# Where VectorE copies finished attention outputs out of PSUM, moved one step earlier in three attention loops

## The reference

```python
# latent attention: 8 heads, two query blocks of 128, causal
s = einsum('bqhd,bkhd->bhqk', q[:, lo:hi], k[:, :hi]) * scale
p = softmax(where(causal, s, NEG_BIG))
o = einsum('bhqk,bkhd->bqhd', p, v[:, :hi])

# cross attention, in each of the first two layers: 4 heads, 256 x 256, no mask
s = einsum('bqhd,bmhd->bhqm', q, k_mem) * MEM_HEAD_DIM ** -0.5
o = einsum('bhqm,bmhd->bqhd', softmax(s), v_mem)

# sparse attention (nsa): 16 heads, three branches summed under gates
out = gb[..., 0:1] * o_cmp + gb[..., 1:2] * o_slc + gb[..., 2:3] * o_win
```

## Time and profile before

| | us |
|---|---|
| median of three runs | 3019.53 |
| lowest, highest | 3018.77, 3023.99 |
| the profiled execution's own time | 3018.77 |
| its span, first to last instruction | 3017.1 |
| PE busy | 2875.0 (95%) |
| DVE busy | 2073.7 (69%) |
| ACT busy | 1501.7 (50%) |
| attention loops: latent | about 78 to 106 |
| cross attention, layers 0 and 1 | about 172 to 186 and 566 to 579 |
| nsa | about 2025 to 2093 |

### The profile page before, as it was taken

How to read it: one execution, slowest core, us unless ns; L and a number is a source line. 1 busy time by engine, 2 the same in 40 slices (tenths; PEclk the granted TensorE clock), 3 DMA queues, 4 the chain that set the end, 5 groups by cost and what they waited for, 6 DMA issues and landing times.

```text
span 3017.1 us, 52823 instructions
## 1 busy us (share of the span) xinstructions
PE 2875.0 (95%) x18004; PEld 2567.0 (85%) x18004; DVE 2073.7 (69%) x3647; ACT 1501.7 (50%) x2607; POOL 60.6 (2%) x118
## 2 busy tenths in 40 slices
PE   8889998899999899999999999999899999999998
PEld 6679787798799799999988888776899999988886
DVE  4567975689765678888965555525588879855555
ACT  2444444544534434448964555114344469845544
POOL 0000100011000000000000000000000000000000
PEclk9999999999999999999999999989999999999999
DMA  5439963499763455553345555540445542355553
GB/s 180 126 113 277 354 224 105 120 301 375 249 180 108 136 175 184 181 181 108 101 155 193 194 191 185 128 126 1 147 157 184 182 157 101 105 188 192 192 193 125
DMA packets 310916, 518.35 MB, mean 172 GB/s; under 512 B 37026, under 2 KB 209442, under 8 KB 310179
## 3 DMA queue, kind: packets, MB, share of 16 engines
q1 hardware_dynamic: 294402, 456.78, 47.7%
q0 software_dynamic: 16416, 60.30, 5.6%
HBM read 515.97 MB, written 1.05 MB: 171 GB/s over the span
## 4 chain that ended last, share of the span: by engine, by line
PE 83%; ACT 7%; DVE 4%; issue 3%; DMA 2%; ACTq 1%; SPq 0%; DVEq 0%
PE ps L915 33%; PE ps L846 11%; PE ps L842 11%; PE ps L843 10%; PE ps L893 3%; ACT spread L1869 1%; DMA tile_ring<-mlp_w_in 1%; ACT spread L1875 1%; PE ps L1282 1%; ACT hot_pair L1869 1%; PE ps L1404 1%; PE ps L817 1%; PE ps L1045 1%; PE ps L776 1%; ACT hot_pair L1875 1%
## 5 line engine op out<-in xcount | busy, mean ns | idle before, releaser
L842 PE MATMUL ps<-x_high,w_high 128*128 128x256 f32 x3264 | 815.9, 287 | 21.6 <-DVE x_low L2570 10.6
L843 PE MATMUL ps<-x_low,w_high 128*128 128x256 f32 x3264 | 804.6, 284 | 0.0
L2070 DVE TENSOR_TENSOR w_low<-tile_ring,w_high 128x1024 fp32r<-128x1024 f32 x360 | 441.1, 1225 | 326.1 <-ACT w_high L1701 325.0
L842 PEld LDWEIGHTS ps<-x_high,w_high 128*128 128x128 f32 x3264 | 628.4, 193 | 29.9 <-issue 15.2
L843 PEld LDWEIGHTS ps<-x_low,w_high 128*128 128x128 f32 x3264 | 629.4, 193 | 0.3
L1701 ACT ACTIVATE w_high<-tile_ring 128x1024 fp32r<-128x1024 f32 x360 | 382.5, 1062 | 473.7 <-PE ps L915 473.7
L846 PE MATMUL ps<-x_high,w_low 128*128 128x256 f32 x3264 | 460.5, 284 | 1.4 <-DVE w_low L2846 1.4
L1849 ACT ACTIVATE w_high<-tile_ring 128x1024 fp32r<-128x1024 f32 x256 | 270.1, 1056 | 314.8 <-PE ps L846 314.3
L846 PEld LDWEIGHTS ps<-x_high,w_low 128*128 128x128 f32 x3264 | 423.7, 193 | 1.6 <-DVE w_low L2846 1.6
L915 PE MATMUL ps<-w_high,x_high 128*128 128x512 f32 x1440 | 387.6, 391 | 21.1 <-DVE x_low L2064 21.1
L915 PE MATMUL ps<-w_high,x_low 128*128 128x512 f32 x1440 | 386.6, 390 | 0.0
(11 more groups left out here) (347 smaller groups left out, 3018.3 us busy)
## 6 DMA issues: line engine op xcount, KB each, us to landing
tile_ring<-peer_u SPq DMA_DIRECT2D x256, 512.0 KB, 3.3
tile_ring<-peer_v SPq DMA_DIRECT2D x256, 512.0 KB, 3.3
arena<-mod_w POOLq DMA_DIRECT2D x112, 512.0 KB, 5.7
tile_ring<-mlp_w_in SPq DMA_DIRECT2D x64, 512.0 KB, 5.1
tile_ring<-mlp_w_out SPq DMA_DIRECT2D x64, 512.0 KB, 5.5
tile_ring<-ret_w_in SPq DMA_DIRECT2D x48, 512.0 KB, 3.9
tile_ring<-peer_w_q SPq DMA_DIRECT2D x32, 512.0 KB, 4.0
tile_ring<-sb_w_qkv SPq DMA_DIRECT2D x24, 512.0 KB, 4.2
```

The costliest lines, as they stand in the source:

```text
L842: nc.tensor.matmul(dst, cols, x_high[:, c, :], start=c == 0, stop=False)
L843: nc.tensor.matmul(dst, cols, x_low[:, c, :], start=False, stop=False)
L2070: V.tensor_tensor(w_low[:, k % 2, :], tile_ring[:, k, :], w_high[:, k % 2, :].bitcast(F32), ALU.subtract).then_inc(low_ready, 1)
```

## The change

Three edits, all on VectorE's side. No instruction is added or removed; 20 lifts stand elsewhere in its stream.

```diff
             def attend(n, group, pre, post, out, lift=None):
 
                 for i in range(n + 3):
+                    if i >= 3 and (i - 3) % group == group - 1:
+                        lift_out(out(i - 3))
                     if i < n:
                         pre(i)
                     if 1 <= i <= n:
                         post(i - 1)
-                    if i >= 3 and (i - 3) % group == group - 1:
-                        lift_out(out(i - 3))
                     if lift and 2 <= i < n + 2:
                         lift(i - 2)
...
-            attend_pairs(MLA_H, None, 6, 2, lambda p: V.tensor_copy(oT[:, 2 * p:2 * p + 2, :],
+            attend_pairs(MLA_H, None, 5, 2, lambda p: V.tensor_copy(oT[:, 2 * p:2 * p + 2, :],
...
-            attend_pairs(2 * NSA_H, nsa_gate, 8, 4, lambda k: V.tensor_copy(oT[:, k, :], ps[:, 7, (k % 2) * T:(k % 2 + 1) * T]))
+            attend_pairs(2 * NSA_H, nsa_gate, 7, 4, lambda k: V.tensor_copy(oT[:, k, :], ps[:, 7, (k % 2) * T:(k % 2 + 1) * T]))
```

## The result

The changed kernel takes 3068.99 us (median of four runs, 3066.77 to 3071.31) against 3020.72 us before (four runs): 1.0164 times as long, 95% interval 1.0143 to 1.0184. That is 48 us more, where 22.5 us were predicted, and above the range. The direction was forecast; the clock case was put second and priced at 13 us.

The account below looks back on a forecast made before the run. TensorE, with 83% of the chain of waits, was taken to bound the kernel. Nsa 14.1, latent attention 2.9 and cross attention 5.5 summed to 22.5 us more, forecast 3042 us, 8-in-10 range 3036 to 3056.

Parts of the forecast that it names:

- the clock case: Rival: pauses in nsa let TensorE's clock fall, 4.3 us a group; three low groups give 3055 us; chance 0.26.
- Sum by the order: All three loops: product, lift, maxima and exponentials run one after the other, 22.5 us more at full clock; chance 0.63.
- Its scores thus start at t + 1.96: Nsa: TensorE's scores start 1.96 us after a lift's start t, instead of t - 0.12, 2.08 us later.
- The group takes 9.53 us: Nsa: a full group, lift to lift, takes 9.53 us instead of 7.45.
- Nsa 14.1: Nsa: 6 x 2.08 = 12.48 us by lift 6, then 1.62 us more for item 31's transposes.
- Latent attention 2.9: Latent attention: lift 2, and with it the end, shifts by 1.19 + 1.72 = 2.9 us.
- Cross attention 2.77 each: Each of two cross attention stages: lift 2 comes at 579.44 instead of 576.67, 2.77 us later.
- First lifts unmoved: Every loop: the first lift stays in place, since its product needs only items already ahead of it.
- The row that I had in favour of a fall: Ahead of nsa's loop: TensorE busy 0.90 us of 2 between 2024 and 2026, granted clock 0.50 at 2030.
- Nothing downstream absorbs the shift: Behind the loops: TensorE needs following products at once and weights are prefetched, so the whole shift reaches the total.
- Nsa paid once: Rival: nsa's pipeline catches up after the first group, costing 2.1 + 1.6 us; total 3031; chance 0.07.
- not slower: Rival: products end before VectorE reaches the lifts, bank 7 frees earlier, gain about 2 us, 3017; chance 0.04.

Follow-up runs that it names:

- e9_fill_tail: Full change plus zero matmuls on TensorE in the pauses of all three loops, also before nsa's lift 6; 3047.95 us, ratio 1.0083.
- e2_cross: Kernel before with only the cross attention edit, the lift moved ahead of the maxima; 3030.76 us, ratio 1.0027.
- e4_fill_nsa: Full change plus two zero matmuls on TensorE in nsa behind each product that a lift waits for; 3050.46 us, ratio 1.0108.

## Why the prediction was wrong

- **Sum by the order: right.** "Its scores thus start at t + 1.96": 1.96 in the kernel after. "The group takes 9.53 us": 9.52 in e9_fill_tail, where the clock is 1.00. Nsa 14.1: 14.0. Latent attention 2.9: 2.8 at full clock, 4.3 in the kernel after. Cross attention 2.77 each: 2.77 in the second stage, with its lifts 1.72, 2.77 and 2.77 us later against the first as forecast (1.7, 2.8, 2.8), and 5.72 in the first, where the clock fell. First lifts unmoved: with the clock equal, lift 0 of cross attention comes 6.13 us behind the first maxima in both.
- **The failed step: the clock's rival ranked second and counted for three groups.** Its price a group was right: 9.53 + 4.3 = 13.83 us, measured 13.79 and 13.81. Its extent was not: nsa ran at 0.69 on average and lost 19.9 us (81.52 - 61.64), not 13, and the rival left out the other loops, where it took 3.0 us in the first cross attention and 1.5 in latent attention (13.92 - 12.46). Together 24 us. The forecast of 3042 put the clock's cost at nothing in all loops; that is the term that failed.
- **The argument that failed.** I set nsa's 72% busy share against the 70% of a cross attention that kept 1.00 and so left the clock case second. The busy share of a stage did not decide here. The same cross attention with 8.93 us busy in 14.03 kept 1.00 in one stage and fell in the other, and the two changed places in e2_cross; nsa, with seven pauses filled in e9, kept 1.00. The row that I had in favour of a fall, decides as little: the same pause of 1.1 us stands in the kernel after, and there the clock stayed at 1.00 behind it, through the whole head of nsa. What did speak for it, and what I gave too little weight, is the pauses themselves, six of 2 us in one loop.

```profile
2044.05:2046.05 2.00, 0.89 (x9) 1.00 0.20 72
```

- **What a better ranking would have given, and the luck in it.** With the six groups of nsa at 13.8 us instead of 9.5 the forecast would have been 3042 + 6 x 4.3 = 3068. That this meets 3068.99 would be luck: nsa lost 19.9 us to the clock and not 25.8, and the 4.5 us in the other loops and 5.8 around them are not in that sum.
- **What the page says.** The Trainium skill's "TensorE: Matmul & The Clock Gate", section "A second HAM failure mode: psum-queue depth-cycling", describes a kernel in which TensorE fell idle for short times so often between groups of matmuls that the clock swung between its two levels. By that description the clock case would have come first. The trace agrees in nsa: 0.53, 1.00 and 0.54 within one loop, and 1.00 throughout with the pauses filled. It agrees in part in cross attention, where the clock fell in some traces and kept 1.00 in others.
- **"Nothing downstream absorbs the shift": right on the shift, incomplete on its side effects.** The stretches around the loops took 5.8 us more in sum (10.05 - 4.28), in part by falls of the clock at other places than before, as the 68.91 against 70.53 us behind latent attention. e2_cross shows that this stretch can lose as much with nothing changed in or ahead of it, so what moves these falls stays open.
- **Nsa paid once, not slower: out.** All six groups paid; all eight lifts of nsa waited, each longer than before (3.12 to 6.33 us where the first six waited 2.78 and about 1.80 before, 2.83 against 0.79 at lift 6, 3.89 against 2.74 at lift 7).

## What to carry to other kernels

An instruction that waits on an in-order engine costs nothing as long as nothing behind it is needed; moving it up by one item puts the next item's work behind it, so look at what stands behind a wait and who waits for that before moving it, not at how long the wait is. When a change adds a recurring pause on TensorE in a loop, price it twice, as time and as clock: here six pauses of 2.0 us, one in each group of 9.5 us, cost 12.5 us as time, and the lower clock 19.9 over the whole loop. A pause that can't be removed can be filled with matmuls nobody waits for; in nsa that gave 19.9 us back. The same code ran at either clock in different traces, so a difference of 1.5 to 4.3 us in one stretch of one trace, as behind latent attention or in nsa's head, proves nothing about an edit.

## What was not expected of the hardware

- Work added to TensorE made the program faster: 28 extra matmul records in nsa (378 against 350), and the stage fell from 81.52 to 61.64 us.
- Cross attention with one and the same order took 14.03 us or 16.56 to 16.99, by the clock alone (1.00, 0.79 and 0.75), also in the same stage of builds with the same code up to there (the first stage of the kernel after and of e4_fill_nsa).
- The kernel after varied by 27 us between its executions (3059.37 to 3086.30, 29 of them), the build with pauses partly filled by 23 (3054.94 to 3078.33, five), where the kernel before varied by 10 on one chip (3018.56 to 3028.45, 21).
- The head of nsa takes 17.87 us in some builds and 13.59 in others, with the clock at 0.62 or 1.00, under the same instructions, and behind the same pause of 1.1 us.
